# An even layer's output projection: ScalarE splits weight tiles ahead of input halves and squares, x blocks behind tiles 10, 12 and 14, the V tile split sooner

## The reference

```python
o = jnp.einsum('ble,ed->bld', jnp.concatenate([ya, yb.astype(ya.dtype)], axis=-1), w_out)
x = x + rmsnorm(o, g_post)              # end of the even layer
h = rmsnorm(x, g_pre)                   # beginning of the odd layer
proj = jnp.einsum('bld,de->ble', h, w_in)
q, k, v, z, f_logit = jnp.split(proj, ODD_SPLITS, axis=-1)
```

## Time and profile before

| what | us |
| --- | --- |
| median of 3 runs (1608.19 to 1608.61) | 1608.41 |
| the profiled execution | 1609.01 |
| its span in the profile | 1607.2 |
| PE busy | 1578.2 (98%) |
| DVE busy | 756.8 (47%) |
| ACT busy | 687.8 (43%) |
| POOL busy | 440.4 (27%) |

### The profile page before, as it was taken

How to read it: one execution, slowest core, us unless ns; L and a number is a source line. 1 busy time by engine, 2 the same in 40 slices (tenths; PEclk the granted TensorE clock), 3 DMA queues, 4 the chain that set the end, 5 groups by cost and what they waited for, 6 DMA issues and landing times. The chain is left out here.

```text
span 1607.2 us, 26548 instructions
## 1 busy us (share of the span) xinstructions
PE 1578.2 (98%) x9640; PEld 1443.6 (90%) x9640; DVE 756.8 (47%) x1688; ACT 687.8 (43%) x1323; POOL 440.4 (27%) x252
## 2 busy tenths in 40 slices
PE   7999999999999999999999999999999999999998
PEld 7999999999999999887877898989898999987785
DVE  5546777664762331563042653434343444436433
ACT  6443333232552322544253544545444545455322
POOL 1214543343112111255555231212212222212000
PEclk9999999999999999999999999999999999999999
DMA  5122222112111111145453445512231323114211
GB/s 151 40 70 65 66 73 87 58 58 56 54 40 44 39 53 53 39 151 195 139 187 101 75 78 58 55 48 76 43 73 31 71 46 69 41 61 163 80 70 43
DMA packets 128649, 120.62 MB, mean 75 GB/s; under 512 B 9714, under 2 KB 112532, under 8 KB 128588
## 3 DMA queue, kind: packets, MB, share of 16 engines
q1 hardware_dynamic: 127388, 115.46, 27.5%
q10 hardware_dynamic: 1200, 4.33, 0.7%
HBM read 101.10 MB, written 18.66 MB: 75 GB/s over the span
## 5 line engine op out<-in xcount | busy, mean ns | idle before, releaser
L693 PE MATMUL PB<-HH,WH 128*128 128x352 f32 x1872 | 617.8, 330 | 4.1 <-POOL WL L601 3.5
L693 PE MATMUL PB<-HH,WL 128*128 128x352 f32 x1872 | 601.8, 321 | 0.0
L693 PE MATMUL PB<-HL,WH 128*128 128x352 f32 x1872 | 600.7, 321 | 0.0
L601 POOL TENSOR_TENSOR WL<-WRAW,WH 128x1024 fp32r<-128x1024 f32 x128 | 310.9, 2429 | 643.0 <-ACT WH L1243 628.6
L693 PEld LDWEIGHTS PB<-HH,WH 128*128 128x128 f32 x1872 | 351.4, 188 | 18.5 <-issue 8.0
L693 PEld LDWEIGHTS PB<-HL,WH 128*128 128x128 f32 x1872 | 352.6, 188 | 0.1
L693 PEld LDWEIGHTS PB<-HH,WL 128*128 128x128 f32 x1872 | 351.5, 188 | 0.0
L1243 ACT ACTIVATE WH<-WRAW 128x1024 fp32r<-128x1024 f32 x128 | 135.1, 1056 | 87.4 <-PE PB L693 72.9
L1753 ACT ACTIVATE SB<-SB,small 128x128 f32<-128x128 f32 (+8 forms) x72 | 53.9, 748 | 87.8 <-DVE small L1780 87.8
L693 PE MATMUL PB<-PT,VTOK 128*128 128x128 f32 (+2 forms) x624 | 81.5, 274 | 0.0
L693 PEld LDWEIGHTS PB<-PT,VTOK 128*128 128x128 f32 (+1 forms) x624 | 78.4, 191 | 1.5
(11 more groups left out here) (275 smaller groups left out, 2303.8 us busy)
## 6 DMA issues: line engine op xcount, KB each, us to landing
WRAW<-in_w_out_even_dram SPq DMA_DIRECT2D x48, 512.0 KB, 3.5
WRAW<-in_w_in_even_dram SPq DMA_DIRECT2D x44, 512.0 KB, 3.8
WRAW<-in_w_in_odd_dram SPq DMA_DIRECT2D x32, 512.0 KB, 6.9
ACSB<-acs_rows SPq DMA_DIRECT2D x16, 528.0 KB, 4.9
NFB<-nf_rows SPq DMA_DIRECT2D x8, 656.0 KB, 3.7
XS<-in_x_prompt_dram SPq DMA_DIRECT2D x8, 512.0 KB, 4.9
X<-in_x_prompt_dram SPq DMA_DIRECT2D x8, 512.0 KB, 4.6
x_rows<-X ACTq DMA_DIRECT2D x8, 512.0 KB, 5.3
```

The source lines that it names most:

```text
L601: pool.tensor_tensor(WL[:, slot(w), :, :], WRAW[:, slot(w), :, :], WH[:, slot(w), :, :].bitcast(f32), ALU.subtract).then_inc(S("w_low"), 1)
L693: return pe.matmul(out, lhsT, rhs, start=start, stop=stop)
```

## The change

Four things. ScalarE's eight copies ahead of the loop go; the loop makes five copies instead of four in each of n = 0 to 7, starting with the ninth, so that all 40 are done by n = 7 as before, and the wait for the last ya stands behind the split of tile 2. At n = 15, 31 and 47 the split of tile n + 2 stands behind the first block of squares instead of the second and the first root; for n = 47 this is the split of the V tile, which was made behind `early_chunk(0, True)`. X_LOADS gives 10, 12 and 14 for blocks 0 to 2 instead of 11, 12 and 13. On TensorE the two turns of cached rows move ahead of the last V chunk.

```diff
--- before.py
+++ after.py
@@ -339,7 +339,7 @@
     PASS_COLS = (slice(0, 3 * P), slice(3 * P, 6 * P), slice(6 * P, TOK))
 
 
-    X_LOADS = (11, 12, 13, 18, 20, 22, 34, 38, 40)
+    X_LOADS = (10, 12, 14, 18, 20, 22, 34, 38, 40)
     OG_SPARE = (7, 4)
 
 
@@ -1038,11 +1038,11 @@
         for k in range(KT):
             pe.wait_ge(S("h1_lo"), 17 + k)
             project_chunk(wf, uf, 2, HH, HL, ks=[k])
-        project_chunk(v0, u0, 2, HH, HL)
         pe.wait_ge(S("clf_in"), 16)
         for b in range(2):
             last = turn(PB[3][0:HEADS_C, b * P:(b + 1) * P], CLT[:, b, :])
         last.then_inc(S("clf_turn"), 1)
+        project_chunk(v0, u0, 2, HH, HL)
 
         def turn_lrow():
 
@@ -1574,9 +1574,6 @@
                     split_inputs(i)
         split_high(oe_tile(1))
         load_ln_exp()
-        act.wait_ge(S("ya"), 8)
-        for i in range(8, 16):
-            split_inputs(i)
         for n in range(OE_TILES):
             p, kk = n // OE_K, n % OE_K
             if p == 2:
@@ -1584,17 +1581,18 @@
                     h1_high(i)
             if kk == OE_K - 1:
                 o_squares(3 * p)
+            split_high(oe_tile(n + 2))
+            if kk == OE_K - 1:
                 o_squares(3 * p + 1)
                 o_rstd(3 * p)
-            if n < OE_TILES - 1:
-                split_high(oe_tile(n + 2))
-            if kk == OE_K - 1:
                 o_squares(3 * p + 2)
                 o_rstd(3 * p + 1)
                 o_rstd(3 * p + 2)
+            if n == 0:
+                act.wait_ge(S("ya"), 8)
             if n < 8:
-                for i in range(4):
-                    split_inputs(16 + 4 * n + i)
+                for i in range(5):
+                    split_inputs(8 + 5 * n + i)
             if p > 0 and kk < 3:
                 x1_finish(3 * p - 3 + kk)
 
@@ -1611,7 +1609,6 @@
 
         x1_finish(6)
         early_chunk(0, True)
-        split_high(v0)
         x1_finish(7)
         x1_finish(8)
         early_chunk(1, True)
```

## The result

| | median us | beside the kernel before |
| --- | --- | --- |
| before | 1608.30 (8 runs) | 1 |
| changed | 1613.15 (8 runs, 1611.92 to 1614.28) | 1.0030 [1.0020, 1.0039] |

The change makes the kernel 0.3% slower: 4.7 us above the 1608.41 from which the forecast started. The forecast was 1610.1, with "within 0.2%" (up to 1611.6) as the likeliest of its three outcomes. The time lies inside the range, and inside the likeliest case's own (1606.5 to 1613.5), but 1.5 us beyond that outcome.

The account below looks back on a forecast made before the run. TensorE, busy 98% of the span, was taken as the bound, so only its stalls and low clock could be won. +3.0 - 0.5 - 0.1 - 0.45 - 0.25 = +1.7 us, to 1610.1 for the median; range 1603.5 to 1614.5.

Parts of the forecast that it names:

- within 0.2%: Whole run: no change that a measurement can tell, up to 1611.6 us; chance 0.57, against slower 0.29 and faster 0.14.
- likeliest case: Whole run: late VectorE subtractions delay tile 11's load; +1.7 us to 1610.1, span 1606.5 to 1613.5; chance 0.70.
- Part 1: Tile 2 of the first output projection: the earlier split removes its 2.15 us stall and 1.7 us dip, about 3.9 won.
- Part 2: VectorE's ya subtractions: only four fit a tile between GpSimd's WL, five are given; the last ends at 714.7 us.
- rival (a): GpSimd's WL wait for VectorE's bursts of five at tiles 3, 5 and 8; +6 us, near 1614.5; chance 0.16.
- Rival (b): VectorE keeps pace, the fifth subtraction hidden, ya_lo complete inside tile 9; -4.7 us, near 1603.7; chance 0.14.
- Part 3: x blocks: tile 11's load queues behind SP's wait for ya_lo; stall some 6.5 us, dip 1.7, tile 12 +3.0 us.
- Part 4: Ends of the first two passes: sooner split wins 0.5 us at tile 17 and 0.1 around the 32-row block.
- Part 5: V tile: sooner split starts V 0.45 us sooner; cached-row turns win 0.25 ahead of V's third chunk.

Follow-up runs that it names:

- x_old_places: The changed kernel with the x blocks back behind tiles 11, 12 and 13: 1607.71 us, 0.9992 of the kernel before.
- x_later_alone: The changed kernel with only the x blocks moved, behind tiles 12, 14 and 15: 1605.67 us, 0.9982 of the kernel before.
- v_sooner_alone: The kernel before with only the V tile split sooner, behind the first of the last three blocks of squares: 1611.92 us, ratio 1.0025.
- v_old_place: The changed kernel with the V tile's split back behind the copy of F's first chunk: 1611.25 us, 1.0018 of the kernel before.
- late_x_v_roots: The changed kernel with x blocks behind tiles 12, 14, 15 and the V tile split behind all squares and roots of the last pass: 1602.42 us, ratio 0.9959.
- eight_short: The changed kernel with VectorE's first eight ya subtractions cut to 32 columns: 1613.06 us, 1.0028 of the kernel before.
- x10_alone: The kernel before with only the x blocks moved, behind tiles 10, 12 and 14: 1609.73 us, ratio 1.0001.
- last_eight_short: The changed kernel with VectorE's last eight ya subtractions cut to 32 columns: 1606.53 us, 0.9985 of the kernel before.

## Why the prediction was right, and where it was wrong

**Part 1, right.** Tile 2 waits for nothing and is 2.3 us ahead, tile 3 3.9 us ahead, as forecast (3.9).

**Part 2, right in its end and loose in its reason.** The last subtraction was forecast for 714.7 and came at 714.35. Four a tile was a little low: forty took nine WL, four or five to each. (In the forecast's sum nine overlaps of 0.08 make 714.6, not 714.3; it took 714.7.) And "one is left over each time" suggested that the lag comes from the first tile on; the two runs with short items show that only the last tiles' share holds SP. GpSimd went next at each of its nine turns, so rival (a) does not occur. By the rule of the Trainium skill (SBUF — State Buffer, "Who interferes with whom") the pair of ports is held for a whole instruction and the other engine blocks; the subtraction that takes 2.75 us beside a WL of 2.77 agrees. Why the product at 331.60 waited for a whole burst and these nine WL did not, no run here shows. Rival (b) falls by the 715.03.

**Part 3, the decisive step, right.** Forecast: asked for at 715.1, landing 5.0, a stall of 6.5, a dip of 1.7, tile 12 late by 3.0. Measured, with the 0.68 taken off: 714.75, 4.7, 5.1, 2.4 and 2.8. The stall was smaller by the sooner end of VectorE (0.35), the landing (0.3) and tile 10 itself, which came 0.5 us later than the 713.1 of the sum (713.57). So tile 11 started 0.7 us sooner than forecast (722.99 against 723.7). The dip cost 0.7 us more, since with a wait of 5.14 us the clock stayed down for 6.8 us and not for 3.4. The two cancel: that tile 12 came within 0.2 us of the forecast is luck, that it came late for this reason is not.

**Part 4, near.** From tile 12 to F's first chunk 0.4 us were won (2.78 late to 2.42), 0.6 forecast. The 0.5 us at tile 17 was not won: its wait went, but tile 18's grew from 0.21 to 1.31, because ScalarE makes the split of tile 18 behind the same squares and roots as before. So it is in every profile with this part of the change (1.29 to 1.31) and in none without it (0.20 to 0.21). GpSimd's WL for it took 3.03 us beside a VectorE product, as it had before (3.05). The 32-row block waits 0.7 us more, as forecast (0.6).

So F's first chunk is 2.42 us late, with 2.4 forecast, and up to there the sum stands.

**Part 5, the step that failed.** Forecast for the V tile and the turns: -0.7. Measured: +2.0, which makes the whole difference between +1.7 and the +4.5 of the profiled execution (1614.15 against 1609.01, less the 0.68). The turns gave what was forecast: 0.32 us ahead of V's third chunk instead of 0.54. V's first chunk came 0.58 us later than before, where I had it 0.45 sooner, with no change as the worst end; at 894.6 less the shift it also misses the 893 to 894 that was to show the forecast right. The rows of ScalarE, GpSimd and VectorE show two errors and one omission:

```profile
889.92 1.06 ACT L1243 ACTIVATE WH<-WRAW 128x1024 fp32r<-128x1024 f32 x1 [2.45 <-DMA WRAW<-in_w_in_odd_dram]
...
891.06 2.39 POOL L601 TENSOR_TENSOR WL<-WRAW,WH 128x1024 fp32r<-128x1024 f32 x1 [3.44 <-ACT WH L1243]
...
892.16 1.30 DVE L1773 TENSOR_TENSOR small<-small 128x1 f32<-128x1 f32 x1 [2.71 <-ACT JUNK L1533]
...
894.76 0.30 ACT L1520 ACTIVATE small<-small 32x1 f32<-32x1 f32 x1 [0.60 <-DVE small L1773]
...
897.16 0.44 ACT L1243 ACTIVATE FROW<-PB 8x352 f32<-8x352 f32 x1
```

The same sum on VectorE in the kernel before:

```profile
886.28 0.14 DVE L1776 TENSOR_TENSOR small<-small 128x1 f32<-128x1 f32 x1
```

F's first chunk comes 3.11 us later in absolute time (887.98 against 884.87); that is taken off here. ScalarE stands 2.45 us for the landing, to the 886.8 of the forecast (889.92 less 3.11).

1. The V tile's own WL (891.06 to 893.45) now runs beside VectorE's short chain of sums and residuals. A sum over one column takes 1.30 us, to 893.46, where it took 0.14 in the kernel before, and what follows on VectorE is late with it. ScalarE stands 0.60 us for the next sum before the last root, and the copy of F's first chunk comes 3.9 us later than before (897.16 against 890.12 of the earlier trace rows), not 3.2. The profiles of x_old_places, x_later_alone and v_sooner_alone show the same (a sum of 1.31 to 1.32, a stand of 0.61 to 0.62); those of v_old_place and late_x_v_roots, with V's split in other places, do not (0.14 and none).
2. I let V start 0.3 us behind the start of that copy. The copy lasts 0.44, and V starts 0.14 behind its end. With the 0.7 of the first point that makes up the 1.03 us between forecast and trace.
3. I charged a dip to the stall at tile 11 and none to this place, since its wait was to get shorter. At 1.95 us it came with one, 1.7 us.

I had moved a step that waits for a transfer ahead of a chain of work on the same engine and priced only the wait on that engine, not what the step's follower (WL) does to the next engine.

**The verdict.** The likeliest case was right in mechanism and place, and its sign (slower) too; its size was 2.8 us too small because of one term (1.0 in V's start, 1.7 in the dip behind it), which carried it from "within 0.2%" to just beyond.

## What to carry to other kernels

When one engine is moved ahead, look for who does not move with it: here TensorE won 3.9 us, VectorE kept its pace between GpSimd's tiles, and a queue that waited for VectorE ahead of TensorE's next load handed the win back with 2.8 us on top. A wait belongs behind the loads that the next tiles need; placing three transfers one or two tiles later turned a loss of 0.3% into a gain. Where a step that waits for a transfer is moved ahead of a chain, follow also what it sets off: here the WL behind the split ran beside VectorE's part of that chain and held it.

## What the runs showed of the hardware

**The clock.** Around waits of 5.14, 4.89 and 4.30 us at tile 11 (changed, v_old_place, eight_short) the granted clock was 0.66 over ten microseconds, and around 1.14 and 0.61 (x10_alone, last_eight_short) there was no dip. Behind 2.15 to 2.16 us at tile 2 (before, x10_alone, v_sooner_alone) it was down for 3.4 us each time. A wait near 2 us ahead of V's first chunk came with a clock of 0.83 over ten microseconds in five profiles (1.95 us in the changed kernel, 2.05, 2.06, 2.00 and 1.93 in x_old_places, eight_short, last_eight_short and v_sooner_alone), and with none in one (1.94, x_later_alone). With 1.36 it did not (the earlier trace rows and v_old_place). So the length of the wait alone does not decide near 2 us, and these runs don't show what does; such a wait is best priced as itself plus 1.7 us, with nothing more as the other end.

**The ports.** A VectorE item of 32 columns is held for a GpSimd instruction just as one of 384 is: in eight_short the first of the three short ones at 681.88 took 2.08 us, where four such items that met no WL took 0.49 together (last_eight_short). Shorter items free little as long as one of them meets each WL.
